# Up products of the feed-forwards in 256-column pieces, summed in one place of PSUM

## The reference, cut to what matters

```
x = x + 0.5 * (silu(n @ w_gate) * (n @ w_up)) @ w_down    # twice; n = rmsnorm(x), hidden width 2816
h = h + square(relu(n @ w_up)) @ w_down                   # twice; hidden width 4096
```

## Time and profile before

| | |
|---|---|
| median of 3 runs | 1222.33 us (1221.72 to 1222.93) |
| the profiled execution: its own time | 1222.73 us |
| its span | 1221.0 us |
| instructions PE / PEld | 6823 / 6823 |
| instructions DVE / ACT | 1309 / 965 |
| HBM read, mean rate | 219.52 MB, 181 GB/s |

### The profile page before, as it was taken

One profiled execution on the slowest core, in us unless ns is written; L12 is line 12 of the kernel. 1 busy time (PEld: TensorE's weight loads), 2 busy tenths in 40 slices (PEclk: granted clock), 3 DMA queues, 4 the chain that ended last, 5 costly groups with the idle time before them and its releaser, 6 DMA issues.

```text
span 1221.0 us, 17603 instructions
## 1 busy us (share of the span) xinstructions
PE 1209.9 (99%) x6823; PEld 1033.0 (85%) x6823; DVE 851.5 (70%) x1309; ACT 627.8 (51%) x965; POOL 90.2 (7%) x192
## 2 busy tenths in 40 slices
PE   9999999999999999999999999999999999999998
PEld 8788888898888888888888988888888888888886
DVE  6877767576575668777776767865756676876754
ACT  6544446566544446444456665544447465744443
POOL 2000000121000010000003210000000540000000
PEclk9999999999999999999999999999999999999999
DMA  7766666545754555655565445866553654676640
GB/s 235 226 195 199 196 196 192 177 137 161 253 199 146 173 156 183 220 179 185 193 199 171 125 143 183 275 191 191 189 171 110 176 165 156 208 249 192 192 141 35
DMA packets 174899, 221.74 MB, mean 182 GB/s; under 512 B 9268, under 2 KB 103568, under 8 KB 174816
## 3 DMA queue, kind: packets, MB, share of 16 engines
q1 hardware_dynamic: 173264, 217.09, 56.2%
q0 software_dynamic: 1248, 3.00, 0.9%
q10 hardware_dynamic: 304, 0.53, 0.1%
HBM read 219.52 MB, written 1.06 MB: 181 GB/s over the span
## 4 chain that ended last, share of the span: by engine, by line
PE 96%; DVE 1%; DMA 1%; ACT 1%; issue 0%; SPq 0%; DVEq 0%; ACTq 0%
PE bank L1478 56%; PE bank L1565 22%; PE bank L1572 11%; PE bank L1499 1%; PE bank L1738 1%; PE bank L1721 1%; DMA raw<-in_ff_w_up 1%; PE bank L1698 1%; PE bank L1696 1%; PE bank L1712 0%; DVE w_lo L980 0%; PE bank L1742 0%; PE bank L1689 0%; DVE work L1034 0%; PE bank L1930 0%
## 5 line engine op out<-in xcount | busy, mean ns | idle before, releaser
L980 DVE TENSOR_TENSOR w_lo<-raw,w_hi 128x1024 fp32r<-128x1024 f32 (+1 forms) x448 | 490.9, 1119 | 199.2 <-ACT w_hi L628 198.9
L628 ACT ACTIVATE w_hi<-raw 128x1024 fp32r<-128x1024 f32 (+1 forms) x448 | 422.2, 972 | 274.4 <-PE bank L1572 137.1
L1565 PE MATMUL bank<-xt,w_hi 128*128 128x512 f32 x1216 | 320.8, 396 | 2.7 <-DVE work L1034 1.9
L1565 PEld LDWEIGHTS bank<-xt,w_hi 128*128 128x128 f32 x1216 | 213.9, 188 | 40.6 <-DVE work L1034 1.8
L1572 PEld LDWEIGHTS bank<-xt,w_lo 128*128 128x128 f32 x1216 | 167.6, 188 | 16.9
L1572 PE MATMUL bank<-xt,w_lo 128*128 128x256 f32 x1216 | 170.1, 278 | 0.0
L1478 PE MATMUL bank<-w_hi,xt 128*128 128x512 f32 x512 | 160.7, 395 | 0.0
L1478 PE MATMUL bank<-w_hi,yt_lo 128*128 128x512 f32 x336 | 132.6, 395 | 0.0
L1478 PE MATMUL bank<-w_lo,yt_hi 128*128 128x512 f32 x336 | 131.1, 390 | 0.0
L1478 PE MATMUL bank<-w_hi,yt_hi 128*128 128x512 f32 x336 | 131.1, 390 | 0.0
L1478 PEld LDWEIGHTS bank<-w_hi,xt 128*128 128x128 f32 x512 | 95.0, 188 | 21.9 <-issue 2.1
(11 more groups left out here) (212 smaller groups left out, 1164.6 us busy)
## 6 DMA issues: line engine op xcount, KB each, us to landing
raw<-in_w_up SPq DMA_DIRECT2D x64, 512.0 KB, 4.2
raw<-in_w_down SPq DMA_DIRECT2D x64, 512.0 KB, 4.5
raw<-in_w_in SPq DMA_DIRECT2D x56, 512.0 KB, 4.7
raw<-in_ff_w_gate SPq DMA_DIRECT2D x88, 256.0 KB, 3.7
raw<-in_ff_w_up SPq DMA_DIRECT2D x88, 256.0 KB, 4.7
raw<-in_ff_w_down SPq DMA_DIRECT2D x88, 256.0 KB, 5.1
raw<-in_moba_w_qkv SPq DMA_DIRECT2D x24, 512.0 KB, 3.9
raw<-in_w_o SPq DMA_DIRECT2D x16, 512.0 KB, 3.7
```

The costliest lines, as they stand in the source:

```text
L628: act.activation(w_hi[:, c % RING, 0:w], raw[:, c % RAW, 0:w], ACT.Copy).then_inc(s["hi_ready"], 1)
L980: dve.tensor_tensor(w_lo[:, c % RING, 0:w], raw[:, c % RAW, 0:w], w_hi[:, c % RING, 0:w].bitcast(F32), ALU.subtract).then_inc(s["lo_ready" ...
L1565: ins = pe.matmul(up_banks(m)[q][:], w_h[:, k % 2, q * P:(q + 1) * P], flat(xt[:, k, :, :]), start=k == 0, stop=False, skip_group_check=True)
```

## The change

A pair (q, k) becomes three products of 256 columns into one place: `w_hi` with `xt_hi`, `w_hi` with `xt_lo`, `w_lo` with `xt_hi`. The same weights are loaded twice for the first two. Two column blocks share a bank, so a chunk fills two banks: 0 and 1 for chunk 0, 4 and 5 for odd chunks, 6 and 7 for the other even ones. The up sums no longer have halves to add: DVE multiplies the bank by `rbc` straight away (`ff1`, `ff2`), or takes max(g, 0) into SBUF and multiplies the bank by it (`mlp0`, `mlp1`). In the first unit of chunk m > 2 PE waits once, for the evacuation of chunk m - 2; chunk 2 of `ff1` and `ff2` waits for the copy of `rbc`. PE reports a chunk's sums twice (after q = 1 of the last unit, and at its end) where it was four times.

```diff
--- before.py
+++ after.py
@@ -57,12 +57,12 @@
 
 
 def ff_sems(n):
-    return {"up_done": 3 * n, "g_done": 4 * n, "nrm_done": 2 * n, "act_done": n, "h_done": n, "ht_hi": n, "ht_lo": n,
+    return {"up_done": n, "nrm_done": 2 * n, "act_done": n, "h_done": n, "ht_hi": n, "ht_lo": n,
             "diag_done": 1, "rbc_ready": 1, "rbc_done": 1, "x_done": 4, "units": RING * n}
 
 
 def mlp_sems(n):
-    return {"up_done": 3 * n, "g_done": 4 * n, "h_done": 2 * n, "ht_hi": 2 * n, "ht_lo": 2 * n, "x_done": 4,
+    return {"up_done": n, "g_done": 2 * n, "h_done": 2 * n, "ht_hi": 2 * n, "ht_lo": 2 * n, "x_done": 4,
             "units": RING * n}
 
 
@@ -225,7 +225,7 @@
         c_dram = nc.dram_tensor("c_dram", [HEADS, S], F32, kind="Internal").ap()
 
         bank = [ctx.enter_context(nc.psum_tensor(f"bank{n}", [P, 512], F32)) for n in range(8)]
-        up_bank, t_bank = bank[4:8], bank[6:8]
+        t_bank = bank[6:8]
         q_bank, k_bank, rbc_bank = bank[0], bank[1], bank[4]
 
         def y_bank(phase, pr):
@@ -286,7 +286,12 @@
 
         def up_banks(m):
 
-            return bank[0:4] if m == 0 else up_bank
+            first = 0 if m == 0 else 4 if m % 2 else 6
+            return bank[first:first + 2]
+
+        def up_place(m, q):
+
+            return up_banks(m)[q // 2][:, (q % 2) * S:(q % 2 + 1) * S]
 
         def h_buffers(m):
 
@@ -1026,24 +1031,26 @@
                     lo(c + 5)
                     before()
                     lo(c + 6)
-                    for q in range(4):
-                        if q < 3:
-                            dve.wait_ge(s["up_done"], at(phase, "up_done") + 3 * m + q + 1)
+                    for t in range(2):
+                        if t == 0:
+                            dve.wait_ge(s["up_done"], at(phase, "up_done") + m + 1)
                         else:
                             consumed(dve, b + 3 if m == 0 else c - 1)
-                        dve.tensor_reduce(work[0][:, q // 2, (q % 2) * S:(q % 2 + 1) * S],
-                                          up_banks(m)[q][:].rearrange("p (a b) -> p b a", a=2), AX_X, ALU.add)\
-                            .then_inc(s["g_done"], 1)
-                        if gated and q % 2:
-                            if m == 0 and q == 1:
+                        g = up_banks(m)[t][:]
+                        if gated:
+                            if m == 0 and t == 0:
 
                                 dve.wait_ge(s["rbc_done"], at(phase, "rbc_done") + 1)
-
-                            dve.wait_ge(s["g_done"], at(phase, "g_done") + 4 * m + q + 1)
-                            dve.tensor_tensor(work[1][:, q // 2, :].rearrange("p (a b) -> p a b", a=2),
-                                              work[0][:, q // 2, :].rearrange("p (a b) -> p a b", a=2),
+                            dve.tensor_tensor(work[1][:, t, :].rearrange("p (a b) -> p a b", a=2),
+                                              g.rearrange("p (a b) -> p a b", a=2),
                                               rbc[:].unsqueeze(1).broadcast_to([P, 2, S]), ALU.mult)\
                                 .then_inc(s["nrm_done"], 1)
+                        else:
+
+                            dve.tensor_scalar(work[0][:, t, :], g, 0.0, None, ALU.max).then_inc(s["g_done"], 1)
+                            dve.wait_ge(s["g_done"], at(phase, "g_done") + 2 * m + t + 1)
+                            dve.tensor_tensor(work[1][:, t, :], g, work[0][:, t, :], ALU.mult)\
+                                .then_inc(s["h_done"], 1)
                     if m < n - 1:
                         lo(c + 7)
                     if gated:
@@ -1051,12 +1058,6 @@
                         dve.wait_ge(s["nrm_done"], at(phase, "nrm_done") + 2 * m + 2)
                         dve.tensor_tensor(work[2][:, 1, :], work[2][:, 0, :], work[1][:, 1, :], ALU.mult)\
                             .then_inc(s["h_done"], 1)
-                    else:
-                        for t in range(2):
-
-                            dve.wait_ge(s["g_done"], at(phase, "g_done") + 4 * m + 2 * t + 2)
-                            dve.scalar_tensor_tensor(work[1][:, t, :], work[0][:, t, :], 0.0, work[0][:, t, :],
-                                                     ALU.max, ALU.mult).then_inc(s["h_done"], 1)
                     for u in (8, 9) if m < n - 1 else (7,):
                         lo(c + u)
                     for t in range(1 if gated else 2):
@@ -1538,6 +1539,7 @@
 
 
                 b, gated = at(phase, "units"), phase in ("ff1", "ff2")
+                taken = "nrm_done" if gated else "h_done"
                 tiles_in = 2 if gated else 4
                 parts = 1 if gated else 2
 
@@ -1552,41 +1554,39 @@
                             ready(c + j)
                         if first_wait:
                             first_wait(j)
+                        if j == 0 and m > 2:
+
+                            pe.wait_ge(s[taken], at(phase, taken) + 2 * m - 2)
+                        if j == 0 and m == 2 and gated:
+
+                            pe.wait_ge(s["rbc_done"], at(phase, "rbc_done") + 1)
                         w_h, w_l = slot(c + j, 2, 1024)
 
                         def high(q):
-                            if j == 0 and m == 1 and q == 3 and gated:
-
-                                pe.wait_ge(s["rbc_done"], at(phase, "rbc_done") + 1)
-                            if j == 0 and m > 1:
-
-                                pe.wait_ge(s["g_done"], at(phase, "g_done") + 4 * (m - 1) + q + 1)
                             for k in (2 * j, 2 * j + 1):
-                                ins = pe.matmul(up_banks(m)[q][:], w_h[:, k % 2, q * P:(q + 1) * P],
-                                                flat(xt[:, k, :, :]), start=k == 0, stop=False,
-                                                skip_group_check=True)
-                            return ins
+                                w = w_h[:, k % 2, q * P:(q + 1) * P]
+                                pe.matmul(up_place(m, q), w, xt_hi[:, k, :], start=k == 0 and q % 2 == 0, stop=False,
+                                          skip_group_check=True)
+                                pe.matmul(up_place(m, q), w, xt_lo[:, k, :], start=False, stop=False,
+                                          skip_group_check=True)
 
                         def low(q):
                             for k in (2 * j, 2 * j + 1):
-                                ins = pe.matmul(up_banks(m)[q][:, 0:S], w_l[:, k % 2, q * P:(q + 1) * P],
-                                                xt_hi[:, k, :], start=False, stop=k == KT - 1,
-                                                skip_group_check=True)
+                                ins = pe.matmul(up_place(m, q), w_l[:, k % 2, q * P:(q + 1) * P], xt_hi[:, k, :],
+                                                start=False, stop=k == KT - 1, skip_group_check=True)
                             return ins
 
-                        if j < 3:
+                        if by_parts:
                             for q in range(4):
-                                ins = high(q)
-                            if by_parts:
-                                ready(c + j)
+                                high(q)
+                            ready(c + j)
                             for q in range(4):
                                 ins = low(q)
                         else:
-
                             for q in range(4):
-                                ins = high(q) if q % 2 == 0 else low(q)
-                                ins = low(q) if q % 2 == 0 else high(q)
-                                if q < 3:
+                                high(q)
+                                ins = low(q)
+                                if j == 3 and q == 1:
                                     ins.then_inc(s["up_done"], 1)
                         ins.then_inc(s["used"], 1)
 
@@ -1639,7 +1639,7 @@
                         opening()
                     up(b + RING * m + 4, m + 1)
                     if m == 0:
-                        pe.wait_ge(s["g_done"], at(phase, "g_done") + 4)
+                        pe.wait_ge(s[taken], at(phase, taken) + 2)
                     down(b + RING * m + 8, m, False)
                 if phase == "mlp1":
                     last_down(b + RING * n - 4, n - 1)
```

## The result

The changed kernel takes **1226.49 us** (median of 8 runs, 1225.76 to 1226.61), the kernel before 1222.47 us beside it (8 runs, 1221.72 to 1224.09). The ratio is 1.003, with a 95% interval of 1.002 to 1.0041: slower by some 4 us, where 1212.4 us and a gain were forecast. The profiled execution of the changed kernel took 1226.47 us, with a span of 1224.7.

What follows compares the result with a forecast made beforehand. The prediction took PE, busy for 1209.9 of 1221.0 us, to bound the kernel. From the median of 1222.33 us, -7.3 (products) and -2.6 (opening of `ff1`) gave 1212.4 us, range 1209.5 to 1218.5.

Steps and rivals of the forecast that it cites:

- The high products: Up products with `w_hi`: each of 512 columns becomes two of 256, a triple 340.0 ns against 346.6 a pair; saves 7.3 us.
- the upper bound: Highest price from rows for an up triple: 352.5 ns, from a projection piece with its entry; 7.2 us lost.
- The entry: Passing from a 512-column product into 256-column ones, once a chunk in up; priced at 0.01 us.
- Bank reuse: Opening of `ff1`: up(2) no longer waits for DVE's evacuation thanks to other banks; 2.6 us saved, bounds 0 and 2.6.
- DVE: 152 additions, 96.1 us, go, all beside PE; operations from PSUM cost no more; DVE busy some 75 us less.
- The end of `ff1`: Between last up product and down(10), where DVE's cover is thinnest: the margin of 0.5 us grows, no gap appears.
- the clock: PE's granted clock stays at its full level; leaving it would make the forecast wrong altogether.
- Rival 3: Slower: in runs of 96 small up products, weight loads or instruction supply don't keep up; 117.5 ns each, 1226.9 us, chance 0.07.
- The rule from the page: N / 2.4 + 2.5 ns a product: the split would cost 3.0 us; the prediction held that the trace disagrees.
- rival 2: Splitting up's products gains nothing, only the opening is won: 1219.7 us, or 1222.7 with the page's charge; chance 0.11 (with rival 4).

Runs made afterwards that it cites:

- b_gap0: The kernel before the change with `xt` moved from 192 to 0 bytes (modulo 256, from `w_hi`); 1228.23 us, ratio 1.0041.
- g_dummy512: Changed kernel plus one overwritten 512-column product (`w_hi` with `xt`) ahead of each chunk's up products but the first; 1221.7 us, ratio 0.9991.
- e4_wait_back: Changed kernel with the old wait back: PE waits for the evacuation of chunk m - 1, not m - 2; 1226.9 us, ratio 1.0035.
- e_gap44: Changed kernel with `yt` and `ht` moved from 0 to 32 bytes (modulo 256, from `w_hi`), `xt` left at 192; 1226.96 us, ratio 1.0035.

## Why the prediction was wrong

**The high products (the largest term).** It priced a triple at 340.0 ns, where this kernel has 3 x 117.5 = 352.5: 7.3 us were to be won, some 6.5 were lost. The number was the upper bound it had named ("352.5 ns a triple", "7.2 us lost"), for a reason it hadn't. The step that failed is the reading of the earlier trace rows: "it keeps this pace over 48 products" was true of the run at 268 us and was taken for a property of the form. In its place the runs show that the form has two paces and that a run takes one or the other by what PE did ahead of it: behind down products all 30 chunks take the slow one, and one product of 512 columns put between turns all 30 fast. The chain that the earlier trace rows was chosen from has runs of 5.85 beside those of 5.64, so the price of a triple had two values in the trace of before, 340.0 and 352.9. That the upper bound was worked out from the entry of the one run, 5.64 / 48, and hit the right number, is chance.

**"The up products with 512 columns are slow by some 6 ns for a reason that the trace doesn't name."** That was right, and was the warning: a term of 7.3 us rested on an unnamed cause going away. The down products had already excluded 512 columns as such. The place of `xt` has a part in it: in `b_gap0` the same products take 229.8 in place of 232.6 ns. The rest stays open.

**The entry.** It was taken as 0.01 us a chunk, from `w_lo` products that follow 512-column products *over `xt`*. In the changed kernel up follows down products instead, and no row of before has 256-column up products behind them. `g_dummy512` shows that this is the difference: 0.43 us a chunk (96 x 4.4 ns), not 0.01.

**Bank reuse.** The size was right, 2.5 us against 2.6, and that is in part luck. The doubled banks, to which it was put down, weren't needed: `e4_wait_back` has the old wait and the same opening. It counted on DVE being as late as before (37.24 us), and DVE was 3.2 us earlier.

**DVE.** The maximum from PSUM, without a row before, was priced at 683 to 692 ns. The groups of DVE by line have it at 682, the multiplication from PSUM at 684:

```profile
L1044 DVE TENSOR_TENSOR work<-bank,rbc 128x512 f32<-128x512 f32 x44 | 28.4, 684 | 1.5 <-PE bank L1575 1.4
...
L1052 DVE TENSOR_TENSOR work<-bank,work 128x512 f32<-128x512 f32 x32 | 22.1, 692 | 1.1
L1050 DVE TENSOR_SCALAR work<-bank 128x512 f32<-128x512 f32 x32 | 21.8, 682 | 0.0
```

That DVE's time is off the path held: 67 us less ("some 75") and no wait of PE for it before or after, but for the opening. The end of `ff1` and the clock stayed as said.

**Rival 3** gave the size, 1226.9 us, at 117.5 ns, with a chance of 0.07. Its reason, that loads or supply don't keep up over 96 products, falls with the 96 at 113.3 ns in up(1) of `ff1`, in `e_gap44` and in `g_dummy512`. That its number is near is chance too. A count wouldn't have warned much either: 2 of 24 runs of projections were slow, which is 0.08, and none of the 24 came behind down products (four came behind other products of 512 columns, and were fast).

**The rule from the page.** The Trainium skill, "TensorE: Matmul & The Clock Gate", section "Back-to-back issue gap", gives N / 2.4 + 2.5 ns for a product by itself and says that a stream of loads and products goes otherwise. The prediction took it for the stream, so the 1222.7 us of rival 2 isn't what the page says of this kernel.

**What stays open.** What PE or SBUF carries over from the products ahead, and why only some products switch it: one of 128 columns does so between up(0) and up(1) of `mlp0` and `mlp1`, but not behind down products or in up(1) of `ff1`. Which reads meet in SBUF at which places. Why the same projections are slow at other points of the kernel before and of the changed one (2 and 3 of 24). Whether fast up and fast down can be had together without the extra product: no place among those tried has both, and `xt` at 160 wasn't tried.

## What to carry to other kernels

Before a price is taken from a stretch of the trace, list every run of that form in the trace: if the same code shows two values, the price is a range between them. How often each occurs there says little of a place with other products ahead, so look for a run with the same ones. Where a gain rests on a slowness that the trace doesn't explain, its chance is no better than the explanation. And when products that follow one another change, look at the first product of a run and at the addresses of the operands before the count of instructions.

## What the runs showed of the hardware that was not expected

- With `xt` at 192, products of 256 columns with a weight load each have two paces, 113.3 and 117.8 ns, at a granted clock of full level throughout. Behind its first few products every run of 24 to 168 in these traces keeps one of the two, unless another product or a drain stands inside it. The products of 512 columns in down take 227 or 233 ns on average.
- The paces depend on the operands' places in SBUF: `yt` and `ht` moved by 32 bytes cost down 6 ns a product, `xt` moved from 192 to any of four other places costs the projections 3.7 to 5.7 ns.
- One product of 512 columns over `xt`, ahead of 96 of 256, makes each of the 96 faster by 4.4 ns in 32 of 34 places and slower by as much in the other two; in sum it pays for itself.
- At the fast pace two products of 256 columns (226.7) cost what one of 512 does (227). No charge for a second product showed.
